# Gate panels of a gated mixer block computed with features on partitions instead of tokens

## The chip, the cores and the metric

The kernel runs on one core of a Trainium2 chip. The metric is the device time of one execution in microseconds; given are the times of whole executions, and one profiled execution whose trace holds every instruction of every engine. The engines are PE (TensorE, with PEld for its weight loads), DVE (VectorE), ACT (ScalarE), POOL (GpSimd) and SP (SyncE, which issues the loads). Each takes its own instructions strictly in the order in which they are written, and waits on semaphores.

## The reference

A first block (gated linear attention and an MLP with squared ReLU, then a norm) is followed by a second block, which is the one that matters here. x is 256 tokens of 2048 features.

```
xn = rmsnorm(h, norm_gain)
q, k, v, g_sb, x_lru, g_lru = split(xn @ w_in)          # 1024 features each
y_sb  = stick_breaking_attention(q, k, v) * silu(g_sb)
y_lru = rg_lru(conv(x_lru)) * silu(g_lru)
h = h + concat(y_sb, y_lru) @ w_out
```

silu(z) is z * sigmoid(z), computed as z/2 * (1 + tanh(z/2)). Inputs, weights and output are fp32.

## The kernel before

The work is a list of 64 **panels** (`KINDS`), each a product of the 256 tokens with 2048 x 512 weights. Panels 48 to 63 are the second block: x, K, Q, V (two each), then 56 and 57 (kind g, the gate g_sb), 58 and 59 (kind l, the gate g_lru), and 60 to 63 (kind f, the product with w_out). A panel has 8 **chunks** of 256 x 512 weights. Each chunk is loaded into one of four ring slots `raw`; ACT rounds it to `w_hi` (L751) and DVE forms the rest `w_lo` (L1057), because each fp32 product is made of three of reduced precision: hi times hi, hi times lo, lo times hi (L438 to L440). The activations stand in `xa` and `xb`, also as hi and lo, with features on partitions. `split_hi(t, c)` and `split_lo(t, c)` prepare the chunk four ahead and wait for `chunk_used`, since they write the slot that chunk c of panel t has just left.

PE multiplies a panel's chunks one after the other (`multiply`), and `after(t, c)` puts other work between chunks: in panels 55 to 58 the attention of two heads each (logits behind chunk 0, sums behind chunk 3, values behind chunk 5), and the turn of the panel before. ACT and DVE run `before(t, c)` and then the split of chunk c. So at a panel's start each of them first finishes the last split of the panel before, and then reads out that panel.

An ordinary panel puts tokens on partitions: the activation is the stationary operand, the weights are the moving one, and the 512 features fill one PSUM bank for each half of the tokens. Two panels in turn use banks 0, 1 and 2, 3; banks 4 and 5 (`tp`) take transposes, 6 and 7 (`aux`) the attention. For a gate panel, ACT writes z/2 (L826) and tanh(z/2) (L828) with the token's scale as a scalar for each partition, DVE makes the product (L1217), PE turns the result with eight transposes of 128 x 128 behind chunk 2 of the next panel (`turn_panel`, L503), DVE multiplies it with the attention's or the recurrence's output (L1280) into `prod`, ACT rounds it to `xb_hi` (L901) and DVE forms `xb_lo` (L1286), from which the f panels read.

The up panels (kind u, in the MLP) go another way, which the change takes up: `multiply_up` (L462) has the weights as stationary operand and the tokens as moving one. For each 128 x 128 block of weights, w_hi meets hi and lo of the tokens in one matmul of 512 columns, w_lo meets hi in one of 256. A panel needs four banks (its four groups of 128 features), and consecutive up panels alternate between banks 0 to 3 and 4 to 7. ACT copies the second halves of the banks out (L836), DVE adds them to the first halves (L1196). The result has features on partitions, and no turn is needed.

Of the kernel before, what the change touches and what calls it, by code (L numbers as in the profile page):

```python
# [4 lines left out]
F32 = mybir.dt.float32  # L5
# [5 lines left out]
P = 128  # L11
D = 2048
S = 256
# [27 lines left out]
FIRST_DL = KINDS.index("D")  # L41
FIRST_X = KINDS.index("x")
FIRST_F = KINDS.index("f")

# [13 lines left out]
def groups_before(turn):  # L60

    turned = sum(KINDS[q] in "qrouDxKQgl" for q in range(min(turn - 1, PANELS)))
    return CH + (4 if turn > 2 else 0) + 2 * turned
# [4 lines left out]
    return done - CH if done <= groups_before(FIRST_U + 1) else done - CH - 2 * KINDS.count("u")  # L68


def first_bank(t):

    block = (t - FIRST_U) // 8
    in_mlp = FIRST_U <= t < FIRST_X
    if in_mlp and KINDS[t] == "u":
        return 4 * ((t + block + 1) % 2)
    return 2 * (t % 2) + (4 if in_mlp and block % 2 == 0 else 0)
# [17 lines left out]
def gated_block_kernel(nc, weights, x, x_turned, columns, w_gate_low, w_gate_up, gla_b_gate, gla_o_norm,  # L95
                       final_norm, q_norm_gain_2, k_norm_gain_2, lru_w_a_2, lru_w_x_2, out):
    ctx = ExitStack()
    with ctx:
# [3 lines left out]
        def sem(name):  # L102
            return ctx.enter_context(nc.semaphore(name))
# [91 lines left out]
        sp_hi = nc.alloc_sbuf_tensor_at("sp_hi", [P, 2, 384], F32R, offset=arena_at + 4 * 15616)  # L195
        sp_lo = nc.alloc_sbuf_tensor_at("sp_lo", [P, 2, 384], F32R, offset=arena_at + 4 * 14592)
        wts = room(11776, 2, 384)
        zt2 = room(12544, TT, N)
        prod = room(13568, 2, N)
        sq2 = room(14592, TT, N)  # L200

# [52 lines left out]
        z_ready, ln_out, sp_out = sem("z_ready"), sem("ln_out"), sem("sp_out")  # L254
        lw_ready, w_out_s, y_ready, y_out = sem("lw_ready"), sem("w_out_s"), sem("y_ready"), sem("y_out")
        prod_out = sem("prod_out")
        out_ready, half_done = sem("out_ready"), sem("half_done")
        out_sent = [sem(f"out_sent{i}") for i in range(2)]

# [141 lines left out]
        def _(pe):  # L401
# [3 lines left out]
            def multiply(t, c):  # L405

                if c == 0:

                    if t == FIRST_U:
                        pe.wait_ge(o_read, GH)  # L410
                        pe.wait_ge(tp_lo, groups_before(t))
                    if t >= 2:
                        for s, kinds in ((acc_read_act, "kqvruxKQVgl"), (acc_read_dve, "kqvouDdxKQVf")):
                            pe.wait_ge(s, count(kinds, t - 2))
                first = KINDS[t] != KINDS[t - 1] and KINDS[t] in "oudDxf" or t == 0
                if first:

                    if t == 0:
                        pe.wait_ge(tp_lo, c + 1)
                    else:  # L420
                        src = {"o": FIRST_O - 8 + 1 + 2 * (c // 2), "u": FIRST_U - 4 + c // 2}
                        pe.wait_ge(tp_lo, groups_before(src.get(KINDS[t], t - 4 + c // 2) + 1) + c % 2 + 1)
                pe.wait_ge(lo_ready, CH * t + c + 1)
                if KINDS[t] == "u":
                    multiply_up(t, c).then_inc(chunk_used, 1)
                    return
                for k in range(CK):
                    for tt in range(TT):
                        last = multiply_tile(t, c, k, tt)
                last.then_inc(chunk_used, 1)  # L430
# [24 lines left out]
            def multiply_up(t, c):  # L455

                slot, own = (CH * t + c) % RING, first_bank(t)
                for w, width in ((w_hi, 2 * S), (w_lo, S)):
                    for k in range(CK):
                        kt = CK * c + k  # L460
                        for j in range(N // P):
                            last = pe.matmul(banks[:, own + j, 0:width], w[:, slot, k, j * P:(j + 1) * P],  # L462
                                             xa[:, kt, 0:width // S, :].rearrange("p h (a b) -> p h b a", a=TT),
                                             start=w is w_hi and kt == 0, stop=w is w_lo and kt == KT - 1)
                return last

            def multiply_first():

# [153 lines left out]
            def sb_logits(h0):  # L622

                pair = (h0, h0 + 1)
                if h0 == 0:
                    pe.wait_ge(tp_hi, groups_before(55))
                    pe.wait_ge(tp_lo, groups_before(55))
                else:
                    pe.wait_ge(y_out, h0)
# [37 lines left out]
            def after(t, c):  # L667

                prev = KINDS[t - 1] if t else ""
                late = 6 if prev in "KQ" else 3 if prev == "D" or prev == "r" and t < FIRST_O else 2  # L670
                if t >= 1 and prev in "qrogDxlKQ" and c == late:
                    turn_panel(t)
                if t == 0:
                    if c == 6:
# [62 lines left out]
        def _(act):  # L737
# [51 lines left out]
            def before(t, c):  # L789
# [3 lines left out]
                if c == 0 and t:  # L793
# [12 lines left out]
                    if prev == "v":  # L806
# [7 lines left out]
                        ins.then_inc(acc_read_act, 1)  # L814
                        act.wait_ge(acc_read_act, count("kqvruxKQVgl", q))
                        act.sem_inc(vals_act, 1)
                    if prev in "rgl":
                        panel_done(act, t)
                        half = scl[:, R1H:R1H + 2] if prev == "r" else scl[:, R2H:R2H + 2]
                        tanh_to = th if prev == "r" else stage[:, b, :, :]  # L820
                        z_to = zt if prev == "r" else zt2
                        n_silu = count("rgl", q)
                        if n_silu > 1:
                            act.wait_ge(stage_dve, count("qruDxKQgl", q) - 1)
                        for tt in range(TT):
                            act.activation(z_to[:, tt, :], acc(q, tt), ACT.Copy,  # L826
                                           scale=half[:, tt:tt + 1])
                            last = act.activation(tanh_to[:, tt, :], acc(q, tt), ACT.Tanh,  # L828
                                                  scale=half[:, tt:tt + 1])
                        last.then_inc(silu_act, 1)  # L830
                        act.wait_ge(silu_act, n_silu)
                        act.sem_inc(acc_read_act, 1)
# [49 lines left out]
                if prev and prev in "qroDx" and c == (4 if prev == "D" or prev == "r" and t < FIRST_O else 3):  # L882
                    for g in range(2):
# [9 lines left out]
                        if prev == "x" and g == 0:  # L893
                            if q == FIRST_X + 1:
                                act.wait_ge(conv_ready, 1)
                            move_first(lru_x[:, 0:2, PAD:PAD + S], G)
                if prev and prev in "gl" and c == (7 if q == 57 else 3):
                    for g in range(2):
                        k = 4 * (q - 56) + 2 * g
                        act.wait_ge(prod_out, 2 * (q - 56) + g + 1)  # L900
                        act.activation(xb_hi[:, k:k + 2, :], prod[:, g, :].rearrange("p (a b) -> p a b", b=S),  # L901
                                       ACT.Copy).then_inc(tp_hi, 1)
                if c == 7 and prev and prev in "KQ":
                    k = 4 * ((q - 50) % 2)
                    if prev == "K":
# [138 lines left out]
        def _(dve):  # L1044
# [86 lines left out]
            def before(t, c):  # L1131
# [3 lines left out]
                if c == 0 and t:  # L1135
# [75 lines left out]
                    if prev == "V":  # L1211
                        j = q - 54
                        half_panel(t, v2[:, 1, j * N:(j + 1) * N], scl[:, R2 + 1:R2 + 2])
                        dve.sem_inc(v2_dve, 1)
                    if prev and prev in "gl":
                        dve.wait_ge(silu_act, count("rgl", q))
                        dve.scalar_tensor_tensor(out=stage[:, b, :, :], in0=stage[:, b, :, :], scalar=1.0,  # L1217
                                                 in1=zt2, op0=ALU.add, op1=ALU.mult).then_inc(stage_dve, 1)
                    if prev == "f":
                        j = q - FIRST_F  # L1220
                        if j >= 2:
# [31 lines left out]
                if prev and prev in "qroDx" and c == (4 if prev == "D" or prev == "r" and t < FIRST_O else 3):  # L1253
                    for g in range(2):
# [9 lines left out]
                        if prev == "x" and g == 1:  # L1264
                            if q == FIRST_X:
                                link(dve.memset(lru_x[:, :, 0:PAD], 0.0))
                            move_second(lru_x[:, 2:4, PAD:PAD + S], G)
                if prev and prev in "gl" and c == (7 if q == 57 else 3):

                    mixed = y_t if prev == "g" else lru_h  # L1270
                    k0 = 4 * ((q - 56) % 2)
                    if prev == "g":
                        dve.wait_ge(y_out, k0 + 4)
                    else:
                        dve.wait_ge(lru_done, 2)
                    for g in range(2):
                        dve.wait_ge(tp_ready, turned(groups_before(t) + g + 1))
                        if q > 56:
                            dve.wait_ge(tp_lo, groups_before(t))
                        dve.tensor_tensor(prod[:, g, :], tp[:, g, :],  # L1280
                                          mixed[:, k0 + 2 * g:k0 + 2 * g + 2, :].rearrange("p a b -> p (a b)"),
                                          ALU.mult).then_inc(prod_out, 1)
                    for g in range(2):
                        k = 4 * (q - 56) + 2 * g
                        dve.wait_ge(tp_hi, groups_before(t) + g + 1)
                        dve.tensor_tensor(xb_lo[:, k:k + 2, :], prod[:, g, :].rearrange("p (a b) -> p a b", b=S),  # L1286
                                          xb_hi[:, k:k + 2, :].bitcast(F32), ALU.subtract).then_inc(tp_lo, 1)
                if c == 7 and prev and prev in "KQ":
                    k = 4 * ((q - 50) % 2) + 2
                    if prev == "K":  # L1290
# [189 lines left out]
                if 55 <= t <= 58:  # L1480
# [11 lines left out]
                    if c == 6:  # L1492
                        for hd in (2 * (t - 55), 2 * (t - 55) + 1):
                            dve.wait_ge(y_ready, hd + 1)
                            dve.tensor_copy(y_t[:, hd, P:S], aux[:, hd % 2, 0:P])
                            dve.tensor_copy(y_t[:, hd, 0:P], aux[:, hd % 2, P:S]).then_inc(y_out, 1)

            def run(t):
                for c in range(CH):
                    before(t, c)  # L1500
                    if t < PANELS:
                        split_lo(t, c)

# [19 lines left out]
def lay_out(a):  # L1523
# [17 lines left out]
    for b in range(MLP_BLOCKS):  # L1541
        parts.append(panels(a["mlp_w_up"][0], b * D, 4))
        parts.append(woven(a["mlp_w_down"][0][b * D:(b + 1) * D], 0, 4))
    parts += [woven(in_2, first, 2) for first in (4096, 1024, 0, 2048, 3072, 5120)]
    parts.append(woven(a["w_out_2"][0], 0, 4))

    columns = np.concatenate([np.reshape(a[name], (-1, P)) for name in (
# [28 lines left out]
```

## Time and profile before

| | us |
|---|---|
| median of 3 executions | 1416.55 |
| lowest, highest | 1416.50, 1417.03 |
| the profiled execution | 1416.27 |
| its span in the trace | 1414.5 |
| PE busy in the span | 1408.7 |
| DVE busy, ACT busy | 866.1, 730.0 |

The span is the time from the first to the last instruction in the trace; the profiled execution's own time is 1.8 us longer. Times in rows count from the span's start. A matmul's busy time in a row (0.38 us for 512 columns) includes the way through the array and overlaps the next one, so the distance between starts is what a matmul costs the stream. The same holds in a small way for ACT and DVE.

### The profile page before, as it was taken

To read this page: it belongs to the slowest core of one execution; us is meant where nothing else is said; L and a number is where in the kernel's file an instruction comes from. 1 tells how busy PE (TensorE), PEld (TensorE's weight loads), DVE (VectorE), ACT (ScalarE), POOL (GpSimd) and SP (SyncE) were. 2 spreads that over 40 slices of the span, in tenths; PEclk is the share of its full clock that TensorE was granted. 3 is DMA by queue.
4 is the path that set the end of the run, shared out by engine and by line. 5 is a ranking of instruction groups with operands and counts; after the bars stand their busy time and mean duration, and the time that the engine had idled before them with its cause. 6 is when DMAs were issued, how large, how long until landed. Compare 5 with 4: busy or idle time off the path is not lost. (4 is left out here: it accounts for less than half of the span.)

```text
span 1414.5 us, 17726 instructions
## 1 busy us (share of the span) xinstructions
PE 1408.7 (100%) x7206; PEld 1249.5 (88%) x7206; DVE 866.1 (61%) x915; ACT 730.0 (52%) x873; POOL 25.5 (2%) x46
## 2 busy tenths in 40 slices
PE   9999999999999999999999999999999999999998
PEld 8888888888899889998899888998888888888887
DVE  6766565665666555665566655565666786565654
ACT  6655555555544444454344444445564665666642
POOL 2000000000000000000000000000000001000000
PEclk9999999999999999999999999999999999999999
DMA  9554556566556566566666666565655456545573
GB/s 363 191 173 164 188 172 206 187 226 227 194 194 206 199 204 204 198 203 204 204 200 202 202 202 207 198 203 187 206 192 184 170 180 212 176 150 178 192 230 129
DMA packets 78096, 279.49 MB, mean 198 GB/s; under 512 B 8704, under 2 KB 9728, under 8 KB 77632
## 3 DMA queue, kind: packets, MB, share of 16 engines
q1 hardware_dynamic: 76000, 273.06, 57.5%
q0 software_dynamic: 864, 3.41, 0.7%
q10 hardware_dynamic: 1152, 1.90, 0.4%
q8 instruction: 57, 0.93, 0.3%
q14 instruction: 23, 0.19, 0.0%
HBM read 276.24 MB, written 2.10 MB: 197 GB/s over the span
## 5 line engine op out<-in xcount | busy, mean ns | idle before, releaser
L1057 DVE TENSOR_TENSOR w_lo<-raw,w_hi 128x1024 fp32r<-128x1024 f32 x508 | 619.6, 1224 | 495.1 <-ACT w_hi L751 491.0
L751 ACT ACTIVATE w_hi<-raw 128x1024 fp32r<-128x1024 f32 x508 | 534.7, 1056 | 622.8 <-PE banks L440 435.0
L438 PE MATMUL banks<-w_hi,xb 128*128 128x512 f32 x768 | 291.8, 380 | 0.0
L439 PE MATMUL banks<-w_lo,xb 128*128 128x512 f32 x768 | 291.1, 379 | 0.0
L440 PE MATMUL banks<-w_hi,xb 128*128 128x512 f32 x768 | 291.1, 379 | 0.0
L438 PE MATMUL banks<-w_hi,xa 128*128 128x512 f32 x752 | 288.3, 383 | 0.2 <-DVE w_lo L1057 0.2
L440 PE MATMUL banks<-w_hi,xa 128*128 128x512 f32 x752 | 285.0, 379 | 0.0
L439 PE MATMUL banks<-w_lo,xa 128*128 128x512 f32 x752 | 285.0, 379 | 0.0
L462 PE MATMUL banks<-xa,w_hi 128*128 128x512 f32 x1024 | 242.3, 379 | 0.0
L462 PEld LDWEIGHTS banks<-xa,w_hi 128*128 128x128 f32 x1024 | 184.3, 190 | 20.8
L440 PEld LDWEIGHTS banks<-w_hi,xb 128*128 128x128 f32 x768 | 145.2, 189 | 20.6
L438 PEld LDWEIGHTS banks<-w_hi,xb 128*128 128x128 f32 x768 | 145.2, 189 | 20.3
L439 PEld LDWEIGHTS banks<-w_lo,xb 128*128 128x128 f32 x768 | 145.2, 189 | 20.3
L438 PEld LDWEIGHTS banks<-w_hi,xa 128*128 128x128 f32 x752 | 142.2, 189 | 20.2 <-DVE w_lo L1057 1.0
L440 PEld LDWEIGHTS banks<-w_hi,xa 128*128 128x128 f32 x752 | 142.1, 189 | 20.2
L439 PEld LDWEIGHTS banks<-w_lo,xa 128*128 128x128 f32 x752 | 142.2, 189 | 19.2
L462 PEld LDWEIGHTS banks<-xa,w_lo 128*128 128x128 f32 x1024 | 134.2, 191 | 6.9
L462 PE MATMUL banks<-xa,w_lo 128*128 128x256 f32 x1024 | 134.9, 275 | 0.0
L385 POOL TENSOR_TENSOR rs<-ms,neg_half 128x2 f32<-128x2 f32 (+1 forms) x12 | 15.0, 1248 | 1115.0 <-DVE ms L1097 1115.0
L782 ACT ACTIVATE arena<-h 128x512 f32<-128x512 f32 (+1 forms) x26 | 18.9, 726 | 10.9 <-DVE h L1186 10.4
L1186 DVE SCALAR_TENSOR_TENSOR h<-banks,scl,h 128x512 f32<-128x512 f32 x32 | 22.5, 744 | 0.0
L1251 DVE TENSOR_TENSOR xb<-stage,xb 128x512 fp32r<-128x512 f32 x32 | 20.6, 685 | 0.0
(206 smaller groups left out, 637.5 us busy)
## 6 DMA issues: line engine op xcount, KB each, us to landing
raw<-in_weights SPq DMA_DIRECT2D x511, 512.0 KB, 3.7
h<-in_x SPq DMA_DIRECT2D x2, 1024.0 KB, 9.9
arena<-in_x_turned SPq DMA_DIRECT2D x7, 256.0 KB, 6.3
result<-stage ACTq DMA_DIRECT2D x6, 256.0 KB, 4.6
arena<-in_final_norm POOLq DMA_DIRECT2D x1, 1024.0 KB, 5.9
raw<-in_weights SPq DMA_DIRECT2D x2, 256.0 KB, 5.0
arena<-in_w_gate_up POOLq DMA_DIRECT2D x1, 512.0 KB, 6.9
arena<-in_gla_b_gate POOLq DMA_DIRECT2D x1, 512.0 KB, 8.0
```

The source lines that it names most:

```text
L385: pool.tensor_tensor(rs[:, i, 0:w], ms[:, i, 0:w], neg_half[:, 0:w], ALU.pow)\
L438: pe.matmul(o, xh[:, kt, xs], woven(w_hi, slot, k), start=kt == 0, stop=False)
L439: pe.matmul(o, xh[:, kt, xs], woven(w_lo, slot, k), start=False, stop=False)
L440: return pe.matmul(o, xl[:, kt, xs], woven(w_hi, slot, k), start=False, stop=kt == KT - 1)
L462: last = pe.matmul(banks[:, own + j, 0:width], w[:, slot, k, j * P:(j + 1) * P], xa[:, kt, 0:width // S, :].rearrange("p h (a b) -> p h b ...
L751: act.activation(w_hi[:, n % RING, :, :], raw[:, n % RING, :, :], ACT.Copy)\
L782: act.activation(junk_to, src, ACT.Square, accum_out=sums[:, col:col + 1])\
L1057: dve.tensor_tensor(w_lo[:, n % RING, :, :], raw[:, n % RING, :, :], w_hi[:, n % RING, :, :].bitcast(F32), ALU.subtract).then_inc(lo_ready, 1)
L1186: last = dve.scalar_tensor_tensor(out=hj[:, tt, :], in0=acc(q, tt), scalar=scl[:, RM2 + tt:RM2 + tt + 1], in1=hj[:, tt, :], op0=ALU.mult, ...
L1251: dve.tensor_tensor(xb_lo[:, k:k + 2, :], stage_u(b, g), xb_hi[:, k:k + 2, :].bitcast(F32), ALU.subtract).then_inc(tp_lo, 1)
```

## The change

The weights of the gate panels are laid out as those of the up panels (`panels` instead of `woven`), and `multiply_gate` multiplies them in that form. Banks 6 and 7 are needed by the attention, so that the four accumulators of a panel go through six banks in pairs: 0, 1 and 4, 5 for panel 56; 2, 3 and 0, 1 for 57; 4, 5 and 2, 3 for 58; 0, 1 and 4, 5 for 59 (`GATE_BANKS`). In chunk 0 the first pair is multiplied before the second, each behind its own wait for `gate_read`. The f panels use banks 2, 3 and 0, 1 in turn.

ACT copies each pair's second halves out (`gate_cross`), DVE adds (`gate_read`). The token scale, which used to be a scalar for each partition, now varies along the row: DVE spreads the two scale columns over 128 columns, PE multiplies them with the identity in panel 54 (`turn_scale`, two fp32 matmuls), ACT copies the result to `gate_row`. DVE multiplies by it, ACT takes the tanh in a later chunk, DVE makes silu and the products with the mixer's output still later (`mix_gate`), and the splits into `xb_hi` and `xb_lo` follow. `GATE_STEPS` sets the chunk of each: tanh, mix, split; an 8 is chunk 0 of the next panel.

```
+GATE_BANKS = {56: (0, 4), 57: (2, 0), 58: (4, 2), 59: (0, 4)}
+GATE_STEPS = {57: (5, 6, 7), 58: (5, 7, 8), 59: (1, 2, 3), 60: (1, 2, 3)}
 def first_bank(t):
+    if t >= FIRST_F:
+        return 2 * ((t + 1) % 2)
...
@@ tensor
+                if KINDS[t] in "gl":
+                    multiply_gate(t, c).then_inc(chunk_used, 1)
+                    return
+                if t == FIRST_F and c == 0:
+                    pe.wait_ge(gate_read, 6)
+                if t == FIRST_F + 1 and c == 0:
+                    pe.wait_ge(gate_read, 7)
...
+            def multiply_gate(t, c):
+                slot, prior = (CH * t + c) % RING, 2 * (t - FIRST_G) - 2
+                for pairs in ((0,), (1,)) if c == 0 else ((0, 1),):
+                    if c == 0 and prior + pairs[0] > 0:
+                        pe.wait_ge(gate_read, prior + pairs[0])
+                    for w, width in ((w_hi, 2 * S), (w_lo, S)):
+                        for k in range(CK):
+                            kt = CK * c + k
+                            for pair in pairs:
+                                for i in range(2):
+                                    j = 2 * pair + i
+                                    last = pe.matmul(
+                                        banks[:, GATE_BANKS[t][pair] + i, 0:width], w[:, slot, k, j * P:(j + 1) * P],
+                                        xa[:, kt, 0:width // S, :].rearrange("p h (a b) -> p h b a", a=TT),
+                                        start=w is w_hi and kt == 0, stop=w is w_lo and kt == KT - 1)
+                return last
+            def turn_scale():
+                pe.wait_ge(row_ready, 1)
+                pe.wait_ge(lru_th, 8)
+                for tt in range(TT):
+                    last = pe.matmul(aux[:, 0, tt * P:(tt + 1) * P], row_from[:, tt, :], ident[:, :],
+                                     start=tt == 0, stop=True, skip_group_check=True)
+                last.then_inc(row_turned, 1)
...
-                if t >= 1 and prev in "qrogDxlKQ" and c == late:
+                if t == 54 and c == 3:
+                    turn_scale()
+                if t >= 1 and prev in "qroDxKQ" and c == late:
                     turn_panel(t)
@@ scalar, before(t, c)
+                    if prev in "gl":
+                        panel_done(act, t)
+                        n_gate = q - FIRST_G
...
+                        for pair in range(2):
+                            bank, own = GATE_BANKS[q][pair], slice(2 * pair, 2 * pair + 2)
+                            act.activation(by_tile(stage_z(b)[:, own, :]), unwoven(banks[:, bank:bank + 2, S:2 * S]),
+                                           ACT.Copy).then_inc(gate_cross, 1)
+                        act.wait_ge(gate_cross, 2 * n_gate + 2)
+                        act.sem_inc(acc_read_act, 1)
...
+                if t in GATE_STEPS and c == GATE_STEPS[t][0]:
+                    act.wait_ge(gate_scaled, q - FIRST_G + 1)
+                    act.wait_ge(stage_dve, count("qruDxKQgl", q) - 1)
+                    act.activation(stage_z(b), gate_z, ACT.Tanh).then_inc(silu_act, 1)
@@ vector, before(t, c)
-                    if prev and prev in "gl":
-                        dve.wait_ge(silu_act, count("rgl", q))
-                        dve.scalar_tensor_tensor(out=stage[:, b, :, :], in0=stage[:, b, :, :], scalar=1.0,
-                                                 in1=zt2, op0=ALU.add, op1=ALU.mult).then_inc(stage_dve, 1)
+                    if prev in "gl":
+                        n_gate = q - FIRST_G
+                        for pair in range(2):
+                            bank, own = GATE_BANKS[q][pair], slice(2 * pair, 2 * pair + 2)
+                            dve.wait_ge(gate_cross, 2 * n_gate + pair + 1)
+                            dve.tensor_tensor(by_tile(gate_z[:, own, :]), unwoven(banks[:, bank:bank + 2, 0:S]),
+                                              by_tile(stage_z(b)[:, own, :]), ALU.add).then_inc(gate_read, 1)
...
+                        dve.tensor_tensor(gate_z, gate_z, gate_row.unsqueeze(1).to_broadcast([P, 4, S]), ALU.mult)\
+                            .then_inc(gate_scaled, 1)
...
+            def mix_gate(t, q, b):
+                dve.wait_ge(silu_act, count("rgl", q))
+                dve.scalar_tensor_tensor(out=stage_z(b), in0=stage_z(b), scalar=1.0, in1=gate_z, op0=ALU.add,
+                                         op1=ALU.mult).then_inc(stage_dve, 1)
...
+                for g in range(2):
+                    dve.tensor_tensor(prod[:, g, :].rearrange("p (a b) -> p a b", b=S),
+                                      stage_z(b)[:, 2 * g:2 * g + 2, :],
+                                      mixed[:, k0 + 2 * g:k0 + 2 * g + 2, :], ALU.mult).then_inc(prod_out, 1)
```

PE at the start of panel 57, before: the last matmuls of panel 56, the first of 57 (L438 to L440 repeat, 12 in a chunk), and no wait on the panel before except for its predecessor's banks.

```order
L439 MATMUL banks<-w_lo,xa 128x512
L440 MATMUL banks<-w_hi,xa 128x512
L438 MATMUL banks<-w_hi,xa 128x512 [waits lo_ready,acc_read_dve,acc_read_act]
L439 MATMUL banks<-w_lo,xa 128x512
L440 MATMUL banks<-w_hi,xa 128x512
...
L632 MATMUL banks<-arena 128x256 [waits y_out]
```

PE at the same place, after: L498 is the matmul of `multiply_gate`, L679 the logits behind chunk 0.

```order
L498 MATMUL banks<-xa,w_lo 128x256 x8
L498 MATMUL banks<-xa,w_hi 128x512 [waits lo_ready,acc_read_dve,acc_read_act]
L498 MATMUL banks<-xa,w_hi 128x512 x3
L498 MATMUL banks<-xa,w_lo 128x256 x4
L498 MATMUL banks<-xa,w_hi 128x512 [waits gate_read]
L498 MATMUL banks<-xa,w_hi 128x512 x3
L498 MATMUL banks<-xa,w_lo 128x256 x4
L679 MATMUL banks<-arena 128x256 [waits y_out]
```

The second half of chunk 0 now stands behind a wait for `gate_read`, that is for DVE's add of panel 56.

DVE across the boundary from panel 57 to 58, before: the last copies of attention values (L1496), two splits, and the silu of panel 57 behind ACT's tanh.

```order
L1496 COPY arena<-banks 128x128
L1495 COPY arena<-banks 128x128 [waits y_ready]
L1496 COPY arena<-banks 128x128
L1057 TENSOR_TENSOR w_lo<-raw,w_hi 128x1024 [waits hi_ready] x2
L1217 SCALAR_TENSOR_TENSOR stage<-stage,arena 128x1024 [waits silu_act]
L1057 TENSOR_TENSOR w_lo<-raw,w_hi 128x1024 [waits hi_ready]
```

DVE at the same place, after: L1567 and L1579 are `mix_gate` of panel 56, L1352 its `xb_lo`, L1287 the adds that read the banks of panel 57, L1292 the scale.

```order
L1562 COPY arena<-banks 128x128
L1567 SCALAR_TENSOR_TENSOR stage<-stage,arena 128x1024 [waits silu_act]
L1579 TENSOR_TENSOR arena<-stage,arena 128x512 [waits y_out,stage_dve]
L1579 TENSOR_TENSOR arena<-stage,arena 128x512
L1124 TENSOR_TENSOR w_lo<-raw,w_hi 128x1024 [waits hi_ready]
L1352 TENSOR_TENSOR xb<-arena,xb 128x2x256 [waits tp_hi] x2
L1124 TENSOR_TENSOR w_lo<-raw,w_hi 128x1024 [waits hi_ready]
L1287 TENSOR_TENSOR arena<-banks,stage 128x512 [waits gate_cross] x2
L1292 TENSOR_TENSOR arena<-arena 128x1024 [waits gate_read]
```

The mix, its products and `xb_lo` of panel 56, which stood further ahead in panel 57, moved to its last two chunks, and the reading of the banks follows the last split.

## Rows read from the trace of the kernel before

**Rows 1.** The page: busy time of each engine, granted clock in 40 slices.

```profile
PE 1408.7 (100%) x7206; PEld 1249.5 (88%) x7206; DVE 866.1 (61%) x915; ACT 730.0 (52%) x873; POOL 25.5 (2%) x46
...
PEclk9999999999999999999999999999999999999999
```

**Rows 2.** Waits by engine, whole span for PE; then 1228 to 1350: us in total, times, longest.

```profile
PE banks L723 <- POOL ident L351: 1.6, 1, 1.6
...
PEld banks L647 <- DVE sp_lo L1490: 0.9, 2, 0.4
```

**Rows 3.** Timeline of PE: start us, us, instruction; first matmul of panels 56 to 61.

```profile
1228.63 0.38 PE L438 MATMUL banks<-w_hi,xa 128*128 128x512 f32 x1
...
1253.35 0.38 PE L438 MATMUL banks<-w_hi,xa 128*128 128x512 f32 x1
...
1279.33 0.38 PE L438 MATMUL banks<-w_hi,xa 128*128 128x512 f32 x1
...
1305.30 0.38 PE L438 MATMUL banks<-w_hi,xa 128*128 128x512 f32 x1
...
1327.01 0.38 PE L438 MATMUL banks<-w_hi,xb 128*128 128x512 f32 x1
...
1348.60 0.38 PE L438 MATMUL banks<-w_hi,xb 128*128 128x512 f32 x1
```

**Rows 4.** Timeline of PE around the turn of a panel, 1200 to 1202 us.

```profile
1200.02 0.38 PE L439 MATMUL banks<-w_lo,xa 128*128 128x512 f32 x1
1200.24 0.38 PE L440 MATMUL banks<-w_hi,xa 128*128 128x512 f32 x1
1200.45 1.04 PE L503 MATMUL banks<-ident,stage 128*128 128x128 f32 x8
...
1201.55 0.38 PE L439 MATMUL banks<-w_lo,xa 128*128 128x512 f32 x1
```

**Rows 5.** Timeline of PE: last block of up panels, its start and its end.

```profile
876.03 1.89 PE L462 MATMUL banks<-xa,w_hi 128*128 128x512 f32 x8
...
959.87 0.38 PE L438 MATMUL banks<-w_hi,xb 128*128 128x512 f32 x1
```

**Rows 6.** Timeline of PE: fp32 matmuls of panel 55, then the values block of panel 56.

```profile
1206.94 0.38 PE L634 MATMUL banks<-arena 128*128 128x128 f32 x2
1207.16 0.60 PE L632 MATMUL banks<-arena 128*128 128x256 f32 x2
...
1246.64 0.38 PE L440 MATMUL banks<-w_hi,xa 128*128 128x512 f32 x1
...
1248.38 0.38 PE L439 MATMUL banks<-w_lo,xa 128*128 128x512 f32 x1
```

**Rows 7.** Timeline of PE, ACT and DVE at the end of an up panel.

```profile
730.27 1.03 PE L462 MATMUL banks<-xa,w_hi 128*128 128x512 f32 x4
...
730.53 1.06 ACT L751 ACTIVATE w_hi<-raw 128x1024 fp32r<-128x1024 f32 x1 [1.56 <-PE banks L462]
731.49 1.01 ACT L836 ACTIVATE arena<-banks 128x1024 f32<-128x1024 f32 x1
...
731.62 1.23 DVE L1057 TENSOR_TENSOR w_lo<-raw,w_hi 128x1024 fp32r<-128x1024 f32 x1 [1.39 <-ACT w_hi L751]
732.76 1.22 DVE L1196 TENSOR_TENSOR stage<-banks,arena 128x1024 f32<-128x1024 f32 x1
```

**Rows 8.** Groups of instructions, 1190 to 1414 us: count | busy us, mean ns | idle before.

```profile
L1280 DVE TENSOR_TENSOR arena<-banks,arena 128x512 f32<-128x512 f32 x8 | 5.1, 682 | 0.0
...
L828 ACT ACT_TABLE_LOAD x3 | 3.8, 1283 | 0.0
```

**Rows 9.** Timeline of PE: sums of panel 58 after their wait; start of the span.

```profile
1292.73 0.44 PE L647 MATMUL banks<-sp_hi,below 128*128 128x384 f32 x1
1293.01 0.34 PE L647 MATMUL banks<-sp_lo,below 128*128 128x384 f32 x1
...
1.59 5.45 PE L723 MATMUL banks<-ident 128*128 128x128 f32 x26 [1.59 <-POOL ident L351]
```

## What was predicted, with its working

> **What bounds the kernel now.** I read the page's first two parts first: PE is busy for 1408.7 of 1414.5 us, at a granted clock of 1.00 in every slice, while DVE (61%) and ACT (52%) have room [rows 1]. Then the waits: PE's longest in the whole span is 1.6 us, for the identity at the very start, and between 1228 and 1350 us, where the gate panels run, its weight loads wait 0.9 us for DVE's sp_lo [rows 2]. So PE's own instruction stream is the time. An edit is worth what it takes out of or puts into that stream, and every wait it puts between two matmuls is paid in full unless work stands before it.
>
> The kernel executes in 1416.27 us around a span of 1414.5 us; that execution lies 0.3 us below the median, 1416.55, of the three runs shown. I add the change to the median. This kernel's runs can tell about 0.2%, 2.8 us, from no change.
>
> **The panels that change.** The starts of panels 56 to 61 on PE are 1228.63, 1253.35, 1279.33, 1305.30, 1327.01 and 1348.60 [rows 3], so the lengths are 24.72, 25.98, 25.97, 21.71 and 21.59 us, together 119.97. Matmuls of 512 columns start 0.216 us apart [rows 4], so the 96 of a panel take 20.74. Panel 56 has 3.98 us of attention work besides (panels 57 and 58 too), panels 57 to 60 have one turn each (eight transposes).
>
> *The turns go.* From the L440 before a turn to the L439 after it are 1.31 us, where two plain steps would be 0.43: a turn costs 0.88 us with its refill [rows 4]. Four turns are 3.5. The five panels hold 119.97 - 3 x 24.72 - 2 x 20.74 = 4.33 us beyond product and attention work; the other 0.8 is waiting, 0.38 and 0.37 of it in panels 57 and 58, where the sums wait for sp_lo [rows 2]. I book it as gone: ACT leaves two tanh and their table load out of the boundary, so its softmax does not start later, and PE comes to the sums 2.0 - 0.88 + 0.1 = 1.2 us later than now by the wait below. If it stayed it would cost 0.8. Removed together: 4.33.
>
> *The product the other way round.* The new panels have the form of the up panels: 64 matmuls of 512 columns and 64 of 256, the same columns, but more instructions. The last block of up panels runs from 876.03 to 959.87: 83.84 us for 32 chunks, 2.62 each, against 12 x 0.216 = 2.592 [rows 5]. The eight short ones take 2.62 - 1.73 = 0.89, 0.111 each. That is 0.22 us for a panel, 0.90 for four.
>
> *The scale as a row.* Two fp32 matmuls of 128 columns in panel 54. An fp32 one of 128 columns is two instructions and takes 0.22 us (1206.94 to 1207.16) [rows 6], and leaving the main stream costs about 0.08 as a turn's refill does: 0.5 us. It waits for a DVE copy given out two chunks earlier and for th tiles of panel 52, long done. Bounds 0.3 to 0.7. The row's copy on ACT and its two DVE copies lie beside the product on engines that are busy for 52% and 61% [rows 1], so I cost them at nothing; without that cover they would be some 0.9 us. The wait for row_out, in front of the logits of panel 55, comes three chunks later.
>
> Up to here: -4.33 + 0.90 + 0.5 = **-2.93 us**, if nothing waits.
>
> **The wait that it adds.** Four accumulators a panel in six banks: the second pair of panel 57 goes to banks 0 and 1, which the first pair of panel 56 held to its last matmul. The order shows PE's wait for gate_read after only eight matmuls of chunk 0, and the same at the second pairs of 58 and 59. Behind it in PE's queue stands everything. The cover is four long and four short matmuls: 4 x 0.216 + 4 x 0.111 = 1.31 us. What has to happen in it, from the boundary of an up panel, where ACT and DVE do the same steps [rows 7]: PE starts the next panel at 730.27 (zero). ACT starts at 730.53 the split of the chunk that has just come free, which stands before the evacuation in its queue, and the evacuation at 731.49 (+1.22). DVE starts its half of the split at +1.35 and the add behind it at 732.76, **+2.49**. The add of one pair (128x512) is of the size of L1280, 0.68 [rows 8], so the first pair is read at +3.17; PE takes up 0.05 later and its first matmul after a wait holds 0.1 longer (at 1292.73: 0.44 against 0.34, and the next one 0.28 away instead of 0.17) [rows 9].
> - Start of 57: 3.22 - 1.31 + 0.1 = **2.0 us**. I take DVE to be idle ahead of this boundary, as there.
> - Start of 58: in panel 57 DVE now has, behind split 5, four copies of 128x128 (an estimate from L1280's 0.68 for 512 columns: 0.2 each), the mix (128x1024, 1.23) and two products (of L1280's size, starting 0.60 apart, as each operation overlaps the next by 0.08 [rows 7]) at step 6, then split 6, two xb_lo (0.60 each) at step 7, and the last split. With zero at the end of chunk 5: two chunks and the values (1.31, from 1246.64 to 1248.38 less two steps [rows 6]) put the next panel at 6.55. ACT's tanh with its table load (1.28) [rows 8] stands before split 5, which puts DVE's split at 1.94; copies from 3.08, mix 3.88, products 5.15, split 6.30, xb_lo 7.44, last split 8.64, add 9.78 to 10.46. PE takes up 3.96 after the boundary: 3.96 - 1.31 + 0.1 = **2.75 us**.
> - Start of 59: in panel 58 the mix stands at step 7, directly ahead of the last split: split 6 at 5.28, mix 6.42, products 7.69, last split 8.84, add 9.98 to 10.66, PE at +4.16: **2.95 us**.
> - Starts of 60 and 61 wait for reads that come in the panel before: nothing.
>
> Sum of waits 7.7 us. Its lower bound is three times what the first boundary gives, 1.9 to 2.0: 5.7; its upper bound, with another split of 1.2 us queued ahead of the add at two of them, 9.5. I take 7.7, since the queue's order there is written out and its durations are all in rows.
>
> After a wait three chunks lie ready and PE is the later one, so the ring adds nothing.
>
> **Result of the sum**: 1416.55 - 2.93 + 7.7 = **1421.3 us**.
>
> The page Perfetto Trace Analysis of the Trainium skill (Optimizing Tensor Performance, Matmuls) says that independent groups should rotate through PSUM banks so that the evacuation of one overlaps the next one's matmuls. That is what six accumulators in turns do, and by the rule alone the sum would end at 1413.6; rows 7 speak against it, because the rotation gives 1.31 us of overlap and the evacuation behind the splits needs 3.2.
>
> **The rivals.**
> - *The reads come within the cover* (the other side): the same edits without waits, 1413.6. It decides at 1.31 us after the panel's start. For it: the up panels never wait. Against: they have four other banks to go to, and DVE's add there starts at +2.49. It would need an evacuation that passes the split in both queues. 5%.
> - *Three short waits only*: DVE keeps up in panels 57 and 58, so that each boundary costs 1.9, or ACT's split and copy run in time that I counted twice: waits of 3 to 6 us, 1416.6 to 1419.5. For it: DVE has 39% of the span free [rows 1]. Against: the mix and xb_lo stand at the last two steps. 13%.
> - *The clock falls after the waits.* At the start of the span 26 transposes took 5.45 us, 0.21 each, where a turn's eight take 0.85, 0.10 each [rows 4, 9]: PE at its lower level, 1.2 GHz, after standing idle. If the two longer waits each put PE back there for as long as those 26 took, each loses 2.7 us: 1421.3 + 5.4 = 1426.7, and with one of them 1424. Against: the clock row shows no fall [rows 1], but after the start no wait of 2 us stands in this span. 10%. The Trainium skill, TensorE: Matmul & The Clock Gate (Why this matters for your kernels), warns of throughput drops from idle gaps between bursts of matmuls; no row of this trace decides whether these are long enough.
> - *The turns were not worth what I took*, or the sums' waits stay: +0.3 to +1, inside the forecast's own width.
>
> **How the numbers follow.** Forecast with three waits of 5.9 to 9.5 us: 72%, 1419.5 to 1423.1. Short waits 13%, no waits 5%, clock 10%. The range 1418.6 to 1424.0 holds the forecast, the upper part of the short waits and the milder clock case, some 84%. Faster by over 0.2% (below 1413.7): 4%. Within 0.2% (up to 1419.4): 13%. Slower: 83%.
>
> **What the changed profile would show.** No transposes behind panels 56 to 59; a PE wait released by DVE's add in the first chunk of panels 57, 58 and 59, of 2.0, 2.75 and 2.95 us, each after eight matmuls; chunks of 2.62 us; panel lengths of 24.9, 26.9, 27.7, 23.9 and 20.7; no wait at sp_lo; the granted clock at 1.00. I am wrong if the waits are absent, if their releaser is ACT or a DMA, or if time is lost in other panels.

## The result

| | before | changed |
|---|---|---|
| median, us | 1416.59 | 1423.1 |
| lowest, highest | 1416.50, 1417.03 | 1422.31, 1425.05 |
| executions | 5 | 5 |
| profiled execution | 1416.27 | 1422.77 |
| its span | 1414.5 | 1421.0 |

The changed kernel takes 1.0045 times as long (95% interval 1.0035 to 1.0056): it is slower by 6.5 us, where 4.8 were forecast (1421.3, range 1418.6 to 1424.0). Ratios, here and below, leave out two slow executions, one of the version with doubled turns (1640.14 us, mean granted clock 0.85) and one of the kernel before beside it (3863.92 us).

The waits of PE in the profile after (in us: total, times, longest). It answers to [rows 2].

```profile
PE banks L498 <- DVE arena L1287: 7.1, 3, 2.7
PE banks L772 <- POOL ident L363: 1.6, 1, 1.6
PE banks L521 <- ACT w_hi L1101: 0.9, 1, 0.9
```

L498 is the matmul of the gate panels, L1287 the add that reads a pair. The three waits are new, and nothing else on PE is (the third row stands at the start of the span, before the first rounded weights are ready, and varies from one execution to the next). The wait for sp_lo is gone.

The timeline of PE after, at the starts of panels 56, 57, 58 and 59 and behind them (start us, us, instruction, idle time before it and its releaser). It answers to [rows 3].

```profile
1228.88 1.03 PE L498 MATMUL banks<-xa,w_hi 128*128 128x512 f32 x4
...
1253.85 1.03 PE L498 MATMUL banks<-xa,w_hi 128*128 128x512 f32 x4
1254.71 0.61 PE L498 MATMUL banks<-xa,w_lo 128*128 128x256 f32 x4
1257.08 1.13 PE L498 MATMUL banks<-xa,w_hi 128*128 128x512 f32 x4 [1.76 <-DVE arena L1287]
...
1260.04 1.89 PE L498 MATMUL banks<-xa,w_hi 128*128 128x512 f32 x8
...
1280.84 1.03 PE L498 MATMUL banks<-xa,w_hi 128*128 128x512 f32 x4
1281.70 0.61 PE L498 MATMUL banks<-xa,w_lo 128*128 128x256 f32 x4
1284.95 1.34 PE L498 MATMUL banks<-xa,w_hi 128*128 128x512 f32 x4 [2.63 <-DVE arena L1287]
1286.08 1.06 PE L498 MATMUL banks<-xa,w_lo 128*128 128x256 f32 x4
1286.94 1.06 PE L679 MATMUL banks<-arena 128*128 128x256 f32 x2
...
1289.57 1.89 PE L498 MATMUL banks<-xa,w_hi 128*128 128x512 f32 x8
...
1310.38 1.03 PE L498 MATMUL banks<-xa,w_hi 128*128 128x512 f32 x4
...
1314.58 1.13 PE L498 MATMUL banks<-xa,w_hi 128*128 128x512 f32 x4 [2.73 <-DVE arena L1287]
...
1334.33 0.38 PE L457 MATMUL banks<-w_hi,xb 128*128 128x512 f32 x1
```

A panel starts with its first pair; the second would start 1.31 us later. In panel 57 it starts at 1257.08, 1.92 late; with the 0.1 of its first matmul that is 2.02. (The idle time in the row is shorter, since a matmul's busy time reaches past its turn in the stream.) In 58 it starts 2.80 late, 2.91 in all, and in 59 2.89 late, 3.00 in all. The panel lengths are then 24.97, 26.99, 29.54 and 23.95 us, and panel 60 takes 20.74.

What DVE does ahead of the second wait, from split 5 of panel 57 to the adds (PE starts panel 58 at 1280.84):

```profile
1276.33 1.23 DVE L1124 TENSOR_TENSOR w_lo<-raw,w_hi 128x1024 fp32r<-128x1024 f32 x1 [2.09 <-ACT w_hi L800]
...
1278.27 1.22 DVE L1567 SCALAR_TENSOR_TENSOR stage<-stage,arena 128x1024 f32<-128x1024 f32 x1
1279.52 1.29 DVE L1579 TENSOR_TENSOR arena<-stage,arena 128x512 f32<-128x512 f32 x2
1280.73 1.22 DVE L1124 TENSOR_TENSOR w_lo<-raw,w_hi 128x1024 fp32r<-128x1024 f32 x1
1281.87 1.28 DVE L1352 TENSOR_TENSOR xb<-arena,xb 128x512 fp32r<-128x512 f32 x2
1283.07 1.22 DVE L1124 TENSOR_TENSOR w_lo<-raw,w_hi 128x1024 fp32r<-128x1024 f32 x1
1284.21 1.28 DVE L1287 TENSOR_TENSOR arena<-banks,stage 128x512 f32<-128x512 f32 x2
```

From split 5 on DVE is never idle, so what sets the date of the add is its own queue. Counted as in the prediction, from the end of chunk 5 (1280.84 - 6.55 = 1274.29), the mix starts at 3.98, the last split at 8.78 and the add at 9.92, where 3.88, 8.64 and 9.78 were forecast.

Panel 58 holds more than its wait. From the second pair to chunk 1, panel 57 takes 1260.04 - 1257.08 = 2.96 us, panel 58 takes 1289.57 - 1284.95 = 4.62 for the same instructions: 1.66 more. The same two stretches by busy time of each engine (us, PE, PEld, DVE, ACT, POOL, granted clock, DMA) show why: first panel 58 from its second pair to chunk 1, then all of panel 57.

```profile
1284.95:1289.57 4.62, 4.62 (x18) 4.07 (x19) 2.99 (x3) 2.31 (x2) 0.00 (x0) 0.63 0.32 113
...
1253.85:1280.84 26.99, 25.23 (x157) 23.13 (x155) 17.03 (x24) 17.26 (x22) 0.00 (x0) 1.00 0.47 157
```

Behind the wait of 2.91 us the granted clock is 0.63 on average over 4.62 us: PE ran most of it at 1.2 GHz. Behind the 2.02 before it and the 3.00 after it, in this execution, it stayed at 2.4.

The span's 6.5 us, added up: the five panels take 126.19 us against 119.97, +6.22; the scale's product +0.45; the first wait and the slow beginning differ by -0.2.

### The profile page after: what moved, and what is told of

It reads as the page before. It is cut to its first block and busy times, and to the rows that moved or that the text cites. A ratio compares the mean times of both kernels' runs of the same rounds, so it can differ in the third digit from the quotient of the medians.

```text
span 1421.0 us, 17933 instructions
## 1 busy us (share of the span) xinstructions
PE 1407.6 (99%) x7306; PEld 1253.6 (88%) x7306; DVE 875.6 (62%) x929; ACT 727.7 (51%) x869; POOL 25.5 (2%) x46
## 5 line engine op out<-in xcount | busy, mean ns | idle before, releaser
L481 PE MATMUL banks<-xa,w_hi 128*128 128x512 f32 x1024 | 242.3, 380 | 0.0
L457 PE MATMUL banks<-w_hi,xa 128*128 128x512 f32 x624 | 239.3, 383 | 0.2 <-DVE w_lo L1124 0.2
L458 PE MATMUL banks<-w_lo,xa 128*128 128x512 f32 x624 | 236.7, 379 | 0.0
L459 PE MATMUL banks<-w_hi,xa 128*128 128x512 f32 x624 | 236.6, 379 | 0.0
L481 PEld LDWEIGHTS banks<-xa,w_hi 128*128 128x128 f32 x1024 | 184.4, 190 | 20.7
L481 PEld LDWEIGHTS banks<-xa,w_lo 128*128 128x128 f32 x1024 | 134.3, 191 | 6.8
L459 PEld LDWEIGHTS banks<-w_hi,xa 128*128 128x128 f32 x624 | 118.1, 189 | 16.7
L457 PEld LDWEIGHTS banks<-w_hi,xa 128*128 128x128 f32 x624 | 118.1, 189 | 16.5 <-DVE w_lo L1124 0.6
L458 PEld LDWEIGHTS banks<-w_lo,xa 128*128 128x128 f32 x624 | 118.1, 189 | 15.9
L498 PE MATMUL banks<-xa,w_hi 128*128 128x512 f32 x256 | 62.1, 383 | 7.1 <-DVE arena L1287 7.1
L498 PEld LDWEIGHTS banks<-xa,w_hi 128*128 128x128 f32 x256 | 45.8, 190 | 12.6 <-DVE arena L1287 7.7
L498 PEld LDWEIGHTS banks<-xa,w_lo 128*128 128x128 f32 x256 | 34.6, 193 | 2.0
```

The source lines that it names most:

```text
L457: pe.matmul(o, xh[:, kt, xs], woven(w_hi, slot, k), start=kt == 0, stop=False)
L458: pe.matmul(o, xh[:, kt, xs], woven(w_lo, slot, k), start=False, stop=False)
L459: return pe.matmul(o, xl[:, kt, xs], woven(w_hi, slot, k), start=False, stop=kt == KT - 1)
L498: last = pe.matmul(banks[:, GATE_BANKS[t][pair] + i, 0:width], w[:, slot, k, j * P:(j + 1) * P], xa[:, kt, 0:width // S, :].rearrange("p h ...
```

## The experiments

The kernel before ran beside them: 1416.62 us in the median with the first four, 1416.70 with the last two.

**Is the DVE work ahead of the last split what lengthens the second and third wait?** The mixes of panels 56 and 57 move behind the boundary; `gate_zs` has a second z buffer where heads 0 to 3 of q2_t are no longer needed.

```
-GATE_STEPS = {57: (5, 6, 7), 58: (5, 7, 8), 59: (1, 2, 3), 60: (1, 2, 3)}
+GATE_STEPS = {57: (5, 11, 12), 58: (5, 9, 10), 59: (3, 4, 5), 60: (1, 2, 3)}
-        gate_z = room(12544, 4, S)
+        gate_zs = (room(12544, 4, S), room(2048, 4, S))
```

> As the changed kernel, but the mix, its products and xb_lo of panels 56 and 57 are moved from the last two chunks of the next panel to a chunk behind the following boundary (a second z buffer makes room). Nothing is left out. Queue theory: the second and third wait were longer than the first (2.91 and 3.00 against 2.02 us in the trace, with the 0.1 of the first matmul) only because of DVE work ahead of the last split; so all three become 2.0, the sum 6.0 instead of 7.9, and since no wait is longer than 2.0 us the granted clock stays at 1.00 in every execution: 1416.6 - 3.0 + 6.0 = 1419.6 us, with a spread of some 0.5 us. Rival (ACT's tanh with its table load, which stands before split 5 in both, is what delays the second and third): waits stay at 2.0, 2.9 and 3.0 and the time at 1421.5 to 1425.

Measured: 1420.06 us (1419.41 to 1421.79), 1.0025 times the kernel before (1.0014 to 1.0035). PE's timeline at the three second pairs:

```profile
1259.40 1.13 PE L498 MATMUL banks<-xa,w_hi 128*128 128x512 f32 x4 [1.76 <-DVE arena L1287]
...
1286.39 1.13 PE L498 MATMUL banks<-xa,w_hi 128*128 128x512 f32 x4 [1.76 <-DVE arena L1287]
...
1313.39 1.13 PE L498 MATMUL banks<-xa,w_hi 128*128 128x512 f32 x4 [1.76 <-DVE arena L1287]
```

All three are now the first one, 1.76 idle, though ACT's tanh still stands before split 5 of both panels. The rival falls, and the extra 0.9 and 1.0 us are shown to be the mix and the products, at the start of 58 with xb_lo. (The edit also moves ACT's roundings to xb_hi; DVE's rows above, without idle time, leave them no part in the date of the add.) The expectation on the clock missed in one point: it is 0.999 in two of eight executions, the profiled one among them. There the load of x came late: ACT, which rounds x before the first weights, waited 3.53 us for it, against 2.42 in the kernel before. PE stood idle for 2.0 us at the start of the span, and the granted clock fell there, not at the gate panels (mean clock by stretch; then ACT's rounding of x and PE's first product):

```profile
5.00:10.00 5.00, 2.99 (x16) 2.46 (x15) 2.26 (x5) 3.27 (x7) 3.03 (x10) 0.84 1.00 359
10.00:20.00 10.00, 10.00 (x44) 8.59 (x43) 9.68 (x16) 9.01 (x16) 0.53 (x1) 0.91 1.04 398
```

```profile
6.73 0.91 ACT L807 ACTIVATE xa<-arena,par 128x256 fp32r<-128x256 f32 x2 [3.53 <-DMA arena<-in_x_turned]
...
8.30 1.94 PE L521 MATMUL banks<-w_hi,xa 128*128 128x512 f32 x4 [2.01 <-ACT w_hi L1101]
```

**Is it the order in the queues that sets the wait?** ACT's copies and DVE's adds move ahead of the last split.

```
             def run(t):
                 for c in range(CH):
                     before(t, c)
+                    if t < PANELS and KINDS[t] in "gl" and c == 7:
+                        read_early(t)
                     if t < PANELS:
                         split_hi(t, c)
```

> As the changed kernel, but ACT's two copies and DVE's two adds that read a gate panel out stand before the last split of that panel in both queues instead of behind it. Nothing is left out. Queue theory: at the start of 57 the read is then over 1.7 us after the boundary and the wait 0.5; at 58 and 59 the adds still stand behind xb_lo and the mix, waits 1.5 and 1.8; sum 3.8, no fall of the clock: 1417.4 us. Rival (the wait is ruled by something that the order in the queues does not touch, such as the read of a bank that PE fills beside it): waits near 2, 2.9 and 3 as now, 1421.5 to 1425. If a late last split starves the ring, a new PE wait for w_lo shows in chunk 3 of a panel, and the time is above 1418.

Measured: 1418.02 us (1417.31 to 1418.87), 1.0008 times the kernel before (0.9999 to 1.0017). PE's timeline: start of panel 57 with its second pair, then the second pairs of 58 and 59.

```profile
1254.01 1.03 PE L498 MATMUL banks<-xa,w_hi 128*128 128x512 f32 x4
...
1255.58 1.13 PE L498 MATMUL banks<-xa,w_hi 128*128 128x512 f32 x4
...
1282.32 1.13 PE L498 MATMUL banks<-xa,w_hi 128*128 128x512 f32 x4 [1.50 <-DVE arena L1591]
...
1309.15 1.13 PE L498 MATMUL banks<-xa,w_hi 128*128 128x512 f32 x4 [1.60 <-DVE arena L1591]
```

The first wait is 1255.58 - 1254.01 - 1.31 = 0.26, with its slow first matmul 0.4 (expected 0.5). The other two, put on the scale of the changed kernel (there 1.76 idle stood for 2.02), are 1.8 and 1.9 (expected 1.5 and 1.8). The split alone is worth 1.1 to 1.6 us at each boundary. No wait for w_lo came in its place: a split that ends 1.2 us later starves nobody.

**Cover from the other side.** The last chunk of a panel is multiplied pair by pair, and the first pair is read while PE works on the second.

```
-                for pairs in ((0,), (1,)) if c == 0 else ((0, 1),):
+                for pairs in ((0,), (1,)) if c in (0, CH - 1) else ((0, 1),):
...
+                    if c == CH - 1 and pairs == (0,):
+                        last.then_inc(gate_half, 1)
```

> As the changed kernel, but the last chunk of a gate panel is multiplied pair by pair, and the first pair is read out (one copy, one add) before the last split, as soon as its own matmuls are done, 1.3 us before the panel's end. Nothing is left out. Queue theory: no wait at 57; at 58 and 59 DVE comes to the add only behind xb_lo and the mix, waits 1.5 and 1.8: sum 3.3, 1416.9 us. Rival (cover counts, not DVE's queue): all three waits fall by 1.3 to 2.6 us alike, leaving 0, 0.3 and 0.4: 1414.3 us.

Measured: 1417.73 us (1417.18 to 1420.14), 1.0007 times (0.9998 to 1.0016). PE's waits in 1220 to 1400 us:

```profile
PE banks L499 <- DVE arena L1603: 3.1, 2, 1.6
```

The first boundary has no wait left, and the other two are those of the version above (1.50 and 1.60 idle), although the first pair was complete 1.3 us earlier. So where DVE is behind, cover on PE's side is worth nothing. The time is 0.8 us above the expected 1416.9. The two waits are together 0.3 longer than expected. The profiled execution (1418.27) lost another 1.2 us far ahead of the gate panels, in a matmul of the RG-LRU that waited for ACT's tanh; ACT had stood 2.83 us waiting for the weights of a chunk.

```profile
1140.46 1.06 ACT L803 ACTIVATE w_hi<-raw 128x1024 fp32r<-128x1024 f32 x1 [2.83 <-DMA raw<-in_weights]
...
1143.81 1.97 PE L667 MATMUL banks<-arena 128*128 128x256 f32 x8 [1.01 <-ACT arena L1050]
```

The profile of the version with doubled turns has the same wait at the same place (0.97 idle), the other six have none. How many of the other executions have it is not recorded.

**Both edits**, the pairs in the last chunk and the mixes behind the boundary:

> Both edits: the last chunk pair by pair with the early read of the first pair, and the mixes moved behind the boundary. Nothing is left out. Queue theory: no wait of PE for gate_read at any boundary, and what is left is the removal of the turns and of the waits for sp_lo, less the short matmuls and the scale: 1416.6 - 4.33 + 0.90 + 0.45 = 1413.6 us, below the kernel before by 0.2%. Rival (the turns and the old waits were not worth 4.3 us on the path): 1415 to 1416.6 with no gate_read wait either. If the waits stay, the queue theory falls.

Measured: 1413.72 us (1413.14 to 1415.49), 0.998 times the kernel before (0.9971 to 0.9989). All of PE's waits in the whole span:

```profile
PE banks L775 <- POOL ident L364: 1.6, 1, 1.6
PE banks L524 <- ACT w_hi L1115: 0.3, 1, 0.3
PE banks L458 <- DVE w_lo L1138: 0.2, 1, 0.2
```

DVE at the boundary between panels 56 and 57 (PE starts 57 at 1254.12): the first add is done 0.56 us after the boundary, the split and the second add follow.

```profile
1254.00 0.68 DVE L1603 TENSOR_TENSOR arena<-banks,stage 128x512 f32<-128x512 f32 x1
1255.47 1.23 DVE L1138 TENSOR_TENSOR w_lo<-raw,w_hi 128x1024 fp32r<-128x1024 f32 x1 [0.79 <-ACT w_hi L803]
1256.62 0.68 DVE L1301 TENSOR_TENSOR arena<-banks,stage 128x512 f32<-128x512 f32 x1
```

This version beats both kernels, by 2.9 us and by 9.4. It also confirms the part of the sum without waits: 1413.6 expected, 1413.7 measured, with a clock of 0.999 or more in all eleven executions.

**Does the clock fall because of the waits?** One more DVE operation between the last split and the adds.

```
                         n_gate = q - FIRST_G
+                        link(dve.tensor_tensor(gate_z, gate_z, gate_z, ALU.max))
                         for pair in range(2):
```

> As the changed kernel, with one more DVE operation of 128x1024 (some 1.25 us, it changes nothing) between the last split and the adds. Both theories see waits of 3.3, 4.1 and 4.2 us, sum 11.6, against 7.9. Clock theory (PE falls to its lower level when it has stood idle for long enough, in the changed kernel in some boundaries of some executions, here in nearly all): beyond 1416.6 - 3.0 + 11.6 = 1425.2 there are 1.7 to 2.7 us for each boundary, 1430 to 1433, and the granted clock is near 0.5 for some 3 us behind every wait. Rival (the fall behind the second wait in the changed kernel's profile has nothing to do with the wait): one fall or none, 1425 to 1428.

Measured: 1430.10 us (1429.31 to 1431.94), 1.0095 times (1.0081 to 1.0109). PE's timeline behind the first wait, behind the second and behind the third:

```profile
1258.83 1.80 PE L498 MATMUL banks<-xa,w_hi 128*128 128x512 f32 x4 [3.02 <-DVE arena L1288]
...
1263.45 1.89 PE L498 MATMUL banks<-xa,w_hi 128*128 128x512 f32 x8
...
1289.62 1.87 PE L498 MATMUL banks<-xa,w_hi 128*128 128x512 f32 x4 [3.89 <-DVE arena L1288]
...
1294.25 1.89 PE L498 MATMUL banks<-xa,w_hi 128*128 128x512 f32 x8
...
1320.52 2.04 PE L498 MATMUL banks<-xa,w_hi 128*128 128x512 f32 x4 [3.99 <-DVE arena L1288]
```

From the second pair to chunk 1 are 4.62 and 4.63 us, where 2.96 is the full rate: 1.66 and 1.67 lost, as once in the changed kernel. The four matmuls behind the third take 2.04 instead of 1.13. So all three waits of the profiled execution are followed by a fall, and 1425.2 + 3 x 1.66 = 1430.2 is the measured time. A fall that costs 1.66 of 1430 us lowers the mean clock by 0.0012; the profiled execution and two others have 0.996, which is three falls, the slowest (1431.94) has 0.995, and the fastest (1429.31) has 0.998, which leaves room for two. The clock theory holds: longer waits bring more falls. My price for a fall was a range, 1.7 to 2.7, and its lower end is right.

**What is a turn worth?** In the kernel before, the eight transposes of each of the four turns are done twice.

```
+                        for k in range(2):
+                            for tt in range(TT):
+                                at = 2 * k + tt
+                                pe.transpose(banks[:, turn_bank(t, g), at * P:(at + 1) * P], src(k, tt), ident[:, :])
                     group(turn_bank(t, g), groups_before(t) + g - 1, src, swapped=int(kind == "Q"))
```

> The kernel before, with each of the eight transposes of panels 56 to 59 done twice (the first copy is overwritten). Turn theory: transposes cost PE 0.10 us each, so four turns cost 3.2 more, but the waits for sp_lo in panels 57 and 58 (0.38 and 0.37) vanish, since PE comes to the sums 0.8 us later: 1416.6 + 3.2 - 0.75 = 1419.0. Rival (those waits follow the turn and stay): 1419.8. If transposes were hidden beside other work: 1416.6.

Measured: 1419.14 us in the median, 1.0017 times (1.0008 to 1.0026), 2.4 us above the kernel before. The only wait left near the gate panels (1228 to 1360 us) is the turn's own, and the groups of four transposes start 0.43 us apart:

```profile
PEld banks L529 <- DVE stage L1224: 0.3, 1, 0.3
```

```profile
1264.08 0.60 PE L529 MATMUL banks<-ident,stage 128*128 128x128 f32 x4
1264.52 0.60 PE L503 MATMUL banks<-ident,stage 128*128 128x128 f32 x4
1264.95 0.60 PE L529 MATMUL banks<-ident,stage 128*128 128x128 f32 x4
```

The waits for sp_lo are absorbed, as expected: they were not the turn's cost but a date set by DVE, at which PE used to be too early. By 32 x 0.109 us the added transposes cost 3.5, of which 0.75 come back in those waits; 2.7 against 2.4 measured. Without the gate's turn these waits need not return either: in the version with both edits PE reaches the sums of panel 57 12.03 us after the panel's start (12.78 before) and still does not wait, since DVE starts the second sp_lo at 10.62 instead of 12.79. There ACT's two tanh and their table load no longer stand at the boundary, ahead of its part of the attention.

## Why the prediction was right

**What bounds the kernel** was read rightly: the profiled spans of the changed kernel and of all six versions are the kernel before's plus what PE's stream gained or lost, within 0.1 us, with the start of the span (-0.2 to +2.1) and the wait of 1.2 us in two of them among the terms.

**The sum without waits**, -2.93 us, was measured at -2.9 by the version with both edits. Its terms: up panels' form +0.25 for a panel (24.97 against 24.72; forecast 0.22), the scale's product 0.45 (0.5), the turns and the old waits gone.

**The waits** of 2.0, 2.75 and 2.95 us came as 2.02, 2.91 and 3.00. The walk through DVE's queue (copies, mix, products, split, xb_lo, last split, add) was also right in its order of causes: moving the mix and xb_lo made all three 2.0, moving the reads ahead of the split took 1.1 to 1.6 off each. Panels 57 and 59 were forecast at 26.9 and 23.9 and took 26.99 and 23.95. The sum of the waits was 7.9 against 7.7. Its upper bound was added up wrongly: 7.7 with another 1.2 at two boundaries is 10.1, not 9.5; the outcome lies below either.

**Where it missed** is the term that it kept out of the sum: it held the fall of the clock for a rival at 10% and priced it at 2.7 us each, two of them or one. The changed kernel's profile shows one fall, of 1.66 us, and its executions have granted clocks of 1.000 at 1422.31, 0.999 at 1422.77 and 1423.19, 0.998 at 1423.1 and 1425.05. At 0.0012 a fall (see the version with longer waits) that is none, one, one, two and two falls. With 1416.6 - 3.0 + 7.9 = 1421.5 for the waits alone, none gives 1421.5, one 1423.2 and two 1424.8; four of the five executions come within 0.8 us of that, the median one (1423.1 with 0.998) lies 1.7 below. So the median is not explained to the last microsecond. That it lies only 1.8 us above the forecast is in part luck: the forecast held no fall, and one costs 1.66 us and not the 2.7 at which I had priced it. Not every fall belongs to a gate panel: the kernel before, which has no such wait, shows 0.999 in 4 of its 30 executions beside the first four versions, up to 1418.83 us, and one version fell at the start of its span. What can be said is that the likely case was the forecast's waits together with a fall, and I should have given it more than half. What I had against it was a trace without any wait of 2 us in it, which is no evidence against a fall behind one of 3.

The medians of the first four versions lie 0.1 to 0.8 us above their expected sums. The profiles show two places outside the gate panels where executions differ, the start of the span (PE's wait for its first rounded weights is between 0.2 and 2.0 us) and the wait of 1.2 us in the RG-LRU. Which of them the unprofiled executions met stays open.

**The rivals.** No waits at all: refuted by the trace, though the version with both edits shows that it was two edits away. Short waits: refuted for this kernel, and true of the two versions that read earlier. Turns worth less: refuted by the doubled turns, within 0.3 us, and by the -2.9 us of the version with both edits.

**The rule of the Trainium skill** on rotating through PSUM banks (Perfetto Trace Analysis, Optimizing Tensor Performance, Matmuls) would have given 1413.6. Six banks for four accumulators do rotate, but what they gave was 1.31 us of overlap for 3.2 us of evacuation and queue; with the evacuation put where the rotation could cover it, the time was 1413.7. The warning of the Trainium skill, TensorE: Matmul & The Clock Gate (Why this matters for your kernels), about idle gaps is borne out by the profiles here: a fall behind each wait of 3.3 to 4.3 us, behind one of the two near 3, behind none of the three of 2.0 among the gate panels.

## What to carry to other kernels

Where fewer spare accumulators than a whole set are rotated, write down the cover in microseconds (the matmuls that can run before the shared bank is needed) and beside it everything that stands ahead of the evacuation in the queues of the engines that read it; here one split of 1.2 us and, later, 3.7 us of unhurried elementwise work decided a change of 3 us. The cure was to finish and read the shared pair first and to move the elementwise work behind the boundary, not to find more banks. And price an idle stretch of PE of about 3 us with the slower matmuls that follow it: here 1.66 us on top.

## What the runs showed of the hardware

- In the profiles, after waits that held PE's dense stream up by 2.91 (changed kernel), 3.3, 4.2 and 4.3 us (one more operation of DVE), its granted clock fell to the lower level and cost 1.66 to 1.67 us each time, the same whatever the wait. Behind the other wait near 3 us of the changed kernel (3.00) it did not fall. Behind 2.0 us it fell at the start of the span, where PE had only run transposes, but not at the gate panels. What decides between these was not settled.
- In a stall PE's idle time in the trace reads 0.16 us less than the delay of the stream, and the first matmul behind it holds 0.1 us longer, so the true cost was 0.26 us above the row (2.02 against 1.76).
- Two fp32 matmuls of 128 columns are four instructions and took 0.37 us, 0.45 with the refill of the stream.
